# Summing the modulation pieces over the partitions with column tiles, contiguous x tiles, and a written-out layer loop

## The reference, cut to what matters

```python
for l in range(2):
    h = rms_norm(x, norm_g[l]);  proj = h @ w_in[l]
    # three attentions: 6 heads "A", 6 heads "B" (low rank), 4 heads "C" (differential)
    # each gated; mixed = concat(a_out, b_out, c_out)
    x = x + mixed @ w_out[l]
x = rms_norm(x, final_norm_g)
```

```python
mod = silu(c) @ w_ada + b_ada         # 8 rows of 2048: six for the layer, two for the end
h = rms_norm(x, g_mix)*(1+scale) + shift; x = x + gate * (attention(h) @ w_out_2)
h = rms_norm(x, g_ffn)*(1+scale2) + shift2; x = x + gate2 * experts(h)   # 32 experts, top 2
out = rms_norm(x, g_final)*(1+scale3) + shift3
```

## Time and profile before

| | us |
|---|---|
| median of 3 runs | 2651.5 (2648.91 to 2654.51) |
| span of the profiled execution | 2647.5 |
| PE busy | 2359.9 (89%) |
| DVE busy | 1420.4 (54%) |
| ACT busy | 727.8 (27%) |

### The profile page before, as it was taken

One profiled execution on the slowest core, in us unless ns is written; L12 is line 12 of the kernel. 1 busy time (PEld: TensorE's weight loads), 2 busy tenths in 40 slices (PEclk: granted clock), 3 DMA queues, 4 the chain that ended last, 5 costly groups with the idle time before them and its releaser, 6 DMA issues. The chain is left out here.

```text
span 2647.5 us, 39689 instructions
## 1 busy us (share of the span) xinstructions
PE 2359.9 (89%) x14916; PEld 1769.8 (67%) x14916; DVE 1420.4 (54%) x2015; ACT 727.8 (27%) x1338; POOL 45.2 (2%) x66
## 2 busy tenths in 40 slices
PE   6999999897999999896999898799988888888886
PEld 6789988786789988786778777454444444444442
DVE  2768797853768697854554453533333333333334
ACT  2433343432433443334554442200000000000001
POOL 0100000000100000002000000000000000000000
PEclk8999999996999999997999998899999999999998
DMA  4877776643877766646433345499999999999997
GB/s 187 302 278 288 277 262 228 259 166 132 325 262 295 272 254 239 257 156 232 142 133 120 130 143 210 162 422 422 422 422 422 422 422 422 422 422 422 422 422 327
DMA packets 110327, 762.76 MB, mean 288 GB/s; under 512 B 13392, under 2 KB 17136, under 8 KB 18416
## 3 DMA queue, kind: packets, MB, share of 16 engines
q1 hardware_dynamic: 110048, 760.21, 72.8%
q10 hardware_dynamic: 144, 0.79, 0.1%
HBM read 758.00 MB, written 2.95 MB: 287 GB/s over the span
## 5 line engine op out<-in xcount | busy, mean ns | idle before, releaser
L2239 PE MATMUL b_ps<-s_raw,s_window 128*64 128x256 f32 x4096 | 461.2, 382 | 58.7 <-DVE x_tokens L2465 39.3
L2239 PEld LDWEIGHTS b_ps<-s_raw,s_window 128*64 128x64 f32 x4096 | 295.3, 137 | 236.2 <-issue 72.9
L1126 DVE TENSOR_TENSOR s_w_tail<-s_raw,s_w_head 128x1024 fp32r<-128x1024 f32 x292 | 346.6, 1225 | 101.0 <-ACT s_w_head L738 100.3
L919 PE MATMUL b_ps<-s_h_head,s_w_head 128*128 128x256 f32 x1184 | 351.0, 296 | 18.3 <-DVE s_w_tail L1126 18.3
L738 ACT ACTIVATE s_w_head<-s_raw 128x1024 fp32r<-128x1024 f32 x292 | 294.2, 1051 | 255.6 <-DMA s_raw<-in_w 182.1
L920 PE MATMUL b_ps<-s_h_tail,s_w_head 128*128 128x256 f32 x1184 | 343.1, 290 | 0.0
L921 PE MATMUL b_ps<-s_h_head,s_w_tail 128*128 128x256 f32 x1184 | 342.5, 289 | 0.0
L1203 DVE SCALAR_TENSOR_TENSOR s_ada_acc<-s_raw,s_c_col,s_ada_acc 128x2048 f32<-128x2048 f32 x120 | 282.4, 2354 | 0.2
L2259 PE MATMUL b_ps<-s_raw,s_diag 128*64 128x512 f32 x1024 | 237.8, 600 | 39.2 <-DMA s_raw<-in_w_down 24.0
L919 PEld LDWEIGHTS b_ps<-s_h_head,s_w_head 128*128 128x128 f32 x1184 | 235.6, 199 | 33.8 <-DVE s_w_tail L1126 23.0
L920 PEld LDWEIGHTS b_ps<-s_h_tail,s_w_head 128*128 128x128 f32 x1184 | 235.7, 199 | 0.1
(11 more groups left out here) (334 smaller groups left out, 3334.3 us busy)
## 6 DMA issues: line engine op xcount, KB each, us to landing
s_raw<-in_w SPq DMA_DIRECT2D x198, 1024.0 KB, 5.0
s_raw<-in_w_ada SPq DMA_DIRECT2D x128, 1024.0 KB, 7.0
s_raw<-in_w_gate SPq DMA_DIRECT2D x128, 1024.0 KB, 24.1
s_raw<-in_w_up SPq DMA_DIRECT2D x128, 1024.0 KB, 26.5
s_raw<-in_w_down SPq DMA_DIRECT2D x128, 1024.0 KB, 26.5
x_tokens<-in_x SPq DMA_DIRECT2D x1, 2048.0 KB, 7.7
s_rel<-in_rel SPq DMA_DIRECT2D x1, 2048.0 KB, 11.4
s_raw<-mod_rows SPq DMA_DIRECT2D x2, 1024.0 KB, 12.3
```

Source lines behind the costliest of these rows:

```text
L919: pe.matmul(out, head, m_head, start=first, stop=False, skip_group_check=True)
L1126: dve.tensor_tensor(w_tail[:, i % SPLITS, cols], raw[:, slot["w", i], cols], w_head[:, i % SPLITS, cols].bitcast(F32), ALU.subtract)\
L2239: ins = pe.matmul(psum[64 * h:64 * h + 64, c // 4, 0:T], window[:, 4 * (c % 4) + k, :], raw[:, c, k * 512 + h * T:k * 512 + h * T + T], st ...
```

## The change

1. The partition sum becomes two steps. `ada_sum`: four matmuls with 32 columns of ones as the stationary operand and 512 contiguous columns of the accumulator as the moving operand, each into its own 32 partitions of one PSUM bank; ACT copies the bank into `ada_acc[:, 0:512]`. `ada_turn`, one piece later: four PE transposes of 128 x 128 from there into PSUM, of which DVE picks one column in 32 and adds the bias. Both use PSUM bank 6.
2. `ada_after` spreads the modulation pieces: 16 pieces, then two steps of the schedule without one. The last one comes at piece 69 instead of 63.
3. The hardware loops over the layers of `first_block` become Python loops: the code of the two layers is written out, waits are against constants, DMA sources are fixed.
4. The feature order changes from k + 16 f to f + 128 k everywhere: x is read in contiguous slices of 128 (`x_tiles`), and the weights, gains, biases and expert weights are laid out to match on the host.
5. `mod` goes to DRAM through a PE transpose and an ACT copy at the start of `second_attention`, so that the DMA writes 128 rows of 512 bytes instead of 1024 of 64 bytes.

```diff
+def ada_after(i):
+    group, k = divmod(i, 18)
+    return 16 * group + k if k < 16 and 16 * group + k < ADA_PIECES else None
...
-        if i < ADA_PIECES:
-            out.append((i, ("ada", i)))
-            if i % 16 == 15:
-                out.append((i + 1, ("ada_sum", i // 16)))
+        a = ada_after(i)
+        if a is not None:
+            out.append((i, ("ada", a)))
+            if a % 16 == 15:
+                out += [(i + 1, ("ada_sum", a // 16)), (i + 2, ("ada_turn", a // 16))]
...
-    x_strided = x[:, :, :].rearrange("p t (f k) -> p t k f", k=KT)
+    x_tiles = x[:, :, :].rearrange("p t (k f) -> p t k f", k=KT)
...
-        with sp.Fori(0, DEPTH) as l:
+        for l in range(DEPTH):
...
-                sp.dma_start(raw[:, n % RAW, :], src[bass.ds(l * count + i, 1), :, :]
-                             .rearrange("a p n -> (a p) n")).then_inc(sem[f"raw{n % RAW}"], 16)
+                sp.dma_start(raw[:, n % RAW, :], src[l * count + i]).then_inc(sem[f"raw{n % RAW}"], 16)
...
+                elif kind == "ada_sum":      # ACT
+                    ps = full(act, s, l)
+                    act.activation(ada_acc[:, 0:512], ps[:, :], ACT.Copy).then_inc(free_sem(s), 1)
...
                     pe.wait_ge(sem["ada_done"], at("ada_done", 16 * s[1] + 15, l))
                     ps = bank_for(pe, s, l)
-                    acc = ada_acc[:, :].rearrange("p (f k) -> p k f", k=KT)
-                    for k in range(KT):
-                        ins = pe.matmul(ps[:, k:k + 1], acc[:, k, :], ones[:, 0:1], start=True, stop=True)
+                    for g in range(4):
+                        ins = pe.matmul(ps[32 * g:32 * g + 32, :], ones[:, 0:32], ada_acc[:, 512 * g:512 * g + 512],
+                                        start=True, stop=True, skip_group_check=True)
+                    ins.then_inc(sem[f"full{bank_of[s]}"], 1)
+                elif kind == "ada_turn":
+                    freed(pe, ("ada_sum", s[1]), l)
+                    ps = bank_for(pe, s, l)
+                    for c in range(4):
+                        ins = pe.transpose(ps[:, c * P:(c + 1) * P], ada_acc[:, c * P:(c + 1) * P], ident)
                     ins.then_inc(sem[f"full{bank_of[s]}"], 1)
...
-                            full(dve, ("ada_sum", j - 1), l)
+                            full(dve, ("ada_turn", j - 1), l)
...
-                elif kind == "ada_sum":      # DVE
+                elif kind == "ada_turn":
                     ps = full(dve, s, l)
-                    at_mod = bass.ds(l * 4 + s[1], 1)
-                    dve.tensor_tensor(mod[:, at_mod, :].rearrange("p a k -> p (a k)"), ps[:, 0:16], ...
+                    at_mod = slice(l * 4 + s[1], l * 4 + s[1] + 1)
+                    dve.tensor_tensor(mod[:, at_mod, :].rearrange("p a (g c) -> p (a g) c", c=4),
+                                      ps[:, :].rearrange("p (c g u) -> p g c u", c=4, g=4)[:, :, :, 0], ...
...
-                sp.dma_start(mod_dram.rearrange("a (p k) -> p a k", p=P), mod[:, :, :])\
-                    .then_inc(sem["mod_out"], 16)
-                sp.wait_ge(sem["mod_out"], 16)
+                sp.wait_ge(sem["mod_rows"], 2)
+                sp.dma_start(mod_dram.rearrange("a (k p) -> (a k) p", p=P), mod_t[:, :])\
+                    .then_inc(sem["mod_rows"], 16)
+                sp.wait_ge(sem["mod_rows"], 18)
...
+        act.wait_ge(sem["mod_rows"], 1)
+        act.activation(mod_t[:, :], psum[7][:, 0:P], ACT.Copy).then_inc(sem["mod_rows"], 1)
...
+        pe.transpose(psum[7][:, 0:P], mod[:, :, :].rearrange("p a k -> p (a k)"), ident).then_inc(sem["mod_rows"], 1)
```

More of the change, by code:

```diff
@@ L172, in first_weights @@
     for l in range(DEPTH):
-        wi = w_in[l].reshape(P, KT, -1)
+        wi = w_in[l].reshape(KT, P, -1).transpose(1, 0, 2)
         for b in range(4):
@@ L235, in first_parameters @@
         put("one_minus", l, 1.0 - lam_init)
-        put("w_f", l, w_in[l][:, 2304:2310].reshape(P, KT * 6))
+        put("w_f", l, w_in[l][:, 2304:2310].reshape(KT, P, 6).transpose(1, 0, 2).reshape(P, KT * 6))
     return par
@@ L377, in psum_plan @@
             n_score += 1
-        elif kind in ("turn", "subnorm", "ada_sum"):
+        elif kind in ("turn", "subnorm", "ada_sum", "ada_turn"):
             take(s, 6)
@@ L437, in first_block @@
         stream.append(("w", i))
-        if i < ADA_PIECES:
-            stream.append(("ada", i))
+        if ada_after(i) is not None:
+            stream.append(("ada", ada_after(i)))
     slot = {piece: n % RAW for n, piece in enumerate(stream)}
@@ L683, in _ @@
         pool.wait_ge(sem["pool_chain"], 1)
-        with pool.Fori(0, DEPTH) as l:
+        for l in range(DEPTH):
             pool.wait_ge(sem["squared"], at("squared", 0, l))
@@ L739, in split_head @@
                    .then_inc(sem["head_split"], 1)
-        with act.Fori(0, DEPTH) as l:
+        for l in range(DEPTH):
             chain = Chain(act, sem["act_chain"], 0, l, ACT_LINKS_1)
@@ L921, in three @@
             return pe.matmul(out, tail, m_head, start=False, stop=last, skip_group_check=True)
-        with pe.Fori(0, DEPTH) as l:
+        for l in range(DEPTH):
             for s in steps:
@@ L1128, in split_tail @@
                    .then_inc(sem["tail_split"], 1)
-        with dve.Fori(0, DEPTH) as l:
+        for l in range(DEPTH):
             chain = Chain(dve, sem["dve_chain"], 0, l, DVE_LINKS_1)
@@ L1206, in _ @@
                     ins.then_inc(sem["ada_done"], 1)
[L1207 removed]
+                elif kind == "ada_turn":
                     ps = full(dve, s, l)
[L1209 to L1211 removed]
+                    at_mod = slice(l * 4 + s[1], l * 4 + s[1] + 1)
+                    dve.tensor_tensor(mod[:, at_mod, :].rearrange("p a (g c) -> p (a g) c", c=4),
+                                      ps[:, :].rearrange("p (c g u) -> p g c u", c=4, g=4)[:, :, :, 0],
+                                      ada_bias[:, at_mod, :].rearrange("p a (g c) -> p (a g) c", c=4), ALU.add)\
                        .then_inc(free_sem(s), 1)
@@ L1453, in second_attention @@
     sem = {name: whole.enter_context(nc.semaphore(f"b2_{name}"))
-           for name in list(tally.order) + ["dve_chain", "pool_chain", "consts", "first_normed", "rel_in", "mod_out"]}
+           for name in list(tally.order) + ["dve_chain", "pool_chain", "consts", "first_normed", "rel_in", "mod_rows"]}
     def sb(name, shape, dt=F32):
@@ L2107, in x_heads @@
             for t in range(TT):
-                ins = act.activation(x_head[:, k % X_SPLITS, t, :], x_strided[:, t, k, :], ACT.Copy,
+                ins = act.activation(x_head[:, k % X_SPLITS, t, :], x_tiles[:, t, k, :], ACT.Copy,
                                      scale=rstd[:, t:t + 1])
@@ L2303, in x_tails @@
             for t in range(TT):
-                ins = dve.scalar_tensor_tensor(out=x_tail[:, k % X_SPLITS, t, :], in0=x_strided[:, t, k, :],
+                ins = dve.scalar_tensor_tensor(out=x_tail[:, k % X_SPLITS, t, :], in0=x_tiles[:, t, k, :],
                                                scalar=rstd[:, t:t + 1],
@@ L2486, in second_weights @@
     qa, ka, va, qb, kb, vb = 0, 1024, 1280, 1536, 2560, 3584
-    wi = w_in.reshape(P, KT, -1)
+    wi = w_in.reshape(KT, P, -1).transpose(1, 0, 2)
     pieces = second_schedule()
@@ L2517 @@
     g_out = np.concatenate([a["g_out_a_2"][0], a["g_out_b_2"][0]])[rows]
-    par2 = np.concatenate([a["g_mix_2"][0].reshape(P, KT), np.broadcast_to(a["sinks_a_2"][0][heads], (P, 16)),
+    par2 = np.concatenate([a["g_mix_2"][0].reshape(KT, P).T, np.broadcast_to(a["sinks_a_2"][0][heads], (P, 16)),
                            g_out.reshape(KT, P).T], 1)
     r_bias = np.concatenate([a["b_router_group_2"][0], a["b_router_expert_2"][0]])
-    par3 = np.concatenate([a["g_ffn_2"][0].reshape(P, KT), np.broadcast_to(np.tile(r_bias, 2), (P, 72))], 1)
-    w_r = np.concatenate([a["w_router_group_2"][0], a["w_router_expert_2"][0]], 1).reshape(P, KT, 36)
+    par3 = np.concatenate([a["g_ffn_2"][0].reshape(KT, P).T, np.broadcast_to(np.tile(r_bias, 2), (P, 72))], 1)
+    w_r = np.concatenate([a["w_router_group_2"][0], a["w_router_expert_2"][0]], 1).reshape(KT, P, 36)\
+        .transpose(1, 0, 2)
     i = np.arange(P)
@@ L2530 @@
                             a["w_ada_final_2"].reshape(KT, P, 2, D).transpose(2, 0, 1, 3)]).reshape(8 * KT, P, D)
-    b_ada = np.concatenate([a["b_ada_2"][0], a["b_ada_final_2"]]).reshape(8, P, KT).transpose(1, 0, 2)
+    b_ada = np.concatenate([a["b_ada_2"][0], a["b_ada_final_2"]]).reshape(8, KT, P).transpose(2, 0, 1)
     arrays = {
```

20 lines of the change are left out of this document (10 added, 10 removed).

## The result

The kernel after ("after" below) takes 2554.3 us (median of 4 runs, 2550.7 to 2558.8) against 2650.2: ratio 0.9638, 95% interval 0.9623 to 0.9654. A second set of five rounds gave 2555.5 us, ratio 0.9649 (0.9635 to 0.9662). The profiled execution has a span of 2548.9 us against 2647.5.

What follows compares the result with a forecast made beforehand. PE was taken to bound the part before 1689 us, DMA the fixed expert stretch after. Terms -74.3 + 20.4 + 0 - 16.3 - 1 - 3 = -74.2 took 2651.5 to 2577 us; range 2560 to 2595.

Steps and rivals of the forecast that it cites:

- Sums added: New partition sums on PE: 2.1 us for five serial steps plus 0.45 for transposes; +20.4 us, ends +10.6 and +31.
- half clock: In the norms: contiguous weights win nothing while PE's clock is halved; two norms starting so gain only 3 us each.
- Sums removed: Eight old partition sums leave PE: 54.7 us of their time plus 19.6 of lost clock behind them, -74.3 us.
- switch of tiling mode: Around the new sums: a drain would make +5 us over 16 switches; by the trace row taken, nothing.
- Contiguous x: Four norms with contiguous weights: -16.3 us, ends -8 and -20; strided gather reads by ACT and DVE another -1.
- Pieces spread: Modulation adds moved from C heads to out pieces: -4 us in the heads, +4 beside the out pieces, together 0.
- Written-out layers: At the turn of the layers: SP issues the next weight right behind the parameters, -3 us, ends 0 and -3.6.
- mod to DRAM: Start of second attention: new path for mod, no engine on the path waits for SP; 0, ends -3 and +1.
- the loop of ring, head and tail: Rival in the first part: PE runs up against DVE and the ring of five; +34 us, 2611, chance 0.22 with no-effect rival.
- Straight code didn't starve: Rival in the first part: written-out code stalls on instruction loads; 3.6 us per stall, +52 with 35, 2704, chance 0.04.
- It does what it says: Opposite rival, on sums and norms: sum not shorter, low clock stays; 2610, chance 0.22 together with the ring rival.
- side-by-side case: Rival on the new sums: four tiles overlap, 2 x 0.43 us per sum, and the spread pays; 2562, chance 0.12.

Runs made afterwards that it cites:

- first run: The kernel after with the old partition sum put back: 16 one-column products with strided weights, no ACT copy or transposes; 2610.7 us, ratio 0.9859.
- second run: The kernel after with the old one-column partition sum, but its weights read contiguously; 2586.2 us, ratio 0.9769.
- third run: The kernel after with the sum as four products over the full array into one bank, unable to overlap; 2567.5 us, ratio 0.9687.
- fourth run: The kernel after with strided x again in four norms and gather, matching host layouts and the old mod-to-DRAM pattern; 2578.6 us, ratio 0.9742.

## Why the prediction was wrong

The direction and the place were right; the sum was some 20 us too small. Two steps failed: the five serial steps of 0.43 us in *Sums added* (8 us), and the half clock that was to limit the gain of the contiguous norms (9 us or more). Both erred to the same side. The rest of the difference is no larger than what two medians can differ by.

*Sums removed*: 54.7 of PE and 19.6 of clock, as forecast. The first run gives 6.84 us a sum and 19.3 us of clock when they come back. That the stride sets the 0.214 us was only argued in the prediction; the second run shows it.

*Sums added*: wrong. "5 steps of 0.43 for 8 instructions" is not what four tiles do. The argument that the second instruction of a product waits for the first in the same tile holds, but nothing makes the other tiles wait for it: the lower end of the bounds, 2 x 0.43, was the right one, and that was the rival's mechanism. 1.0 for the eight and 0.6 for the transposes make 8 x 1.6 = 12.8 instead of 20.4. The net term of the sum was -54; it is -57 to -63. The nearest row had already shown two tiles at full overlap.

On the switch of tiling mode the row was nearly right. Starts around the new sum are 0.21 and 0.22 us apart (160.75 to 160.96, 161.96 to 162.18) where they are 0.12 in steady work. Ahead of the sum in the full array (third run) it is 0.12, so 0.09 goes with the tiles there; behind the one-column sum of the second run, which changes no tiling, it is 0.20 too, so the 0.1 behind can't be put down to the switch. A drain such as the Trainium skill states (TensorEngine Tiling, Key Properties) is then a third of the 0.3 that a whole tail would be, or less. The Trainium skill's rule (TensorE: Matmul & The Clock Gate, Part 3) that a pack of column tiles spans about one product agrees with 1.00 us against 2 x 0.43.

*Contiguous x*: wrong in part, 17 with the gather where the fourth run gives 26 (28.5 in the trace). I let the low clock limit the gain ("the other two start on the half clock: -3 each") and did not see that the strided weights are themselves work that lets it fall. The low clock behind them was gone too. By stage the two layers give 11.1 us for my 8.1, the second part 6.8 for my 3, and `experts` with the gather 10.6 for my 6.3. In the norm of the second part DVE paces, as said: it takes its four groups 2.30 us apart without waiting, and PE is ahead of it at 0.111 us per instruction once the clock is at 1.00; with the strided reads DVE waits for PE and the groups are 3.49 us apart.

*Pieces spread*: 0, and 2.4 us measured, which is within the scatter. Both sides are there: 6.6 us gained in the C heads of both layers for my 4, and 3.5 to 6.1 lost over the out pieces for my 4. That they nearly cancel is luck. That DVE is the fuller engine in the C heads was misread: the window of the earlier trace rows took in 10 us of the out pieces, and over the C heads alone PE is.

*Written-out layers*: -3; the turn is that much shorter in the trace. The total can't tell: 2.4 us, with an uncertainty of 6. Its other side, 1.2 us more at the end of the part, I had not seen.

*mod to DRAM*: 0. No run changes it alone. The issue takes 5.49 us instead of 5.07, though the rows are now whole ones of 512 bytes. What waits behind it is the `gate_row` load, which no engine on the path needs there.

*The rivals*: the loop of ring, head and tail did not take over: PE's waits for the tail split are 39 to 40 us, where they were 45.6. What is left of them is in part in the C heads, where more gaps took 6 us off each layer. Straight code didn't starve (76 loads on the queue instead of 80). It does what it says: the sum is shorter and the clock is back. The range missed because it stopped 6 us below the side-by-side case and took that case with the small norm term: the four tiles side by side and the clock behind the norms give 2577 - 8 - 9 = 2560, and the 5 us from there to the measured time are within what two such medians can differ by. So the side-by-side rival had the mechanism of the sum right, and 8 of its 15 us came from there; the 5 that it took from the spread did not come.

## What to carry to other kernels

Price a partition sum by its weight loads: count them, look at the stride of what is loaded, and look at the granted clock behind as well as at the time within. Here one-column products and strided norms both cost once in their own time and once more, a third to two thirds as much, in what followed. Work of another stream that is spread over the steps belongs beside those steps where its engine has room: here six adds per layer taken out of the C heads were worth 11 to 14 us, and six gaps at fixed intervals nothing that could be told. Find the place by the waits and the length of each stage: a mean busy share did not show it, and the sum of the waits over the run did not either.

## What was not expected of the hardware

- A one-column float32 product takes 0.109 us per instruction with contiguous weights (at the full clock) and 0.214 with 64 bytes between elements.
- Eight instructions of 512 float32 columns over four 32-column tiles take 1.06 us with the tail, against 3.60 in the full array.
- The clock falls behind strided norms as well, although each instruction there streams 128 columns: in the second part it is 0.66 over 10 us behind the strided norm and 1.00 behind the contiguous one. It does not stay up everywhere: over the router products it is 0.53 and 0.68.
